# Four column groups for a gate projection, four row groups for the row broadcasts of a head

## The reference

```python
xm, z = jnp.split(h @ w_in, 2, axis=-1)
xc = jax.nn.silu(_conv_centred(xm, conv_w, conv_b))
q = _headwise(xc, wq); k = _headwise(xc, wk); v = _headwise(xm, wv)
gin = jnp.concatenate([q, k, v], axis=-1)
ipre = (jnp.einsum('btc,dch->dbht', gin, w_ig) + b_ig[:, None, :, None]).astype(F32)
lf = jax.nn.log_sigmoid((jnp.einsum('btc,dch->dbht', gin, w_fg) + b_fg[:, None, :, None]).astype(F32))
...
m_t = jnp.maximum(inter, jnp.max(dmat, axis=-1))
s = jnp.einsum('bhtd,bhsd->bhts', qc, kc) * jnp.exp(dmat - m_t[..., None])
w_inter = jnp.exp(inter - m_t)
h = num / jnp.maximum(jnp.abs(den), jnp.exp(-m_t))[..., None]
```

## Time and profile before

| | us |
|---|---|
| median of 3 runs | 1950.06 (1946.19 to 1950.61) |
| span of the profiled execution | 1948.8 |
| PE busy in it | 1816.9 (93%) |
| PE weight loads busy | 1050.9 (54%) |
| DVE, ACT, POOL busy | 604.2, 495.2, 167.7 |
| mean granted clock of PE | 0.968 of full speed |

### The profile page before, as it was taken

How to read it: one execution, slowest core, us unless ns; L and a number is a source line. 1 busy time by engine, 2 the same in 40 slices (tenths; PEclk the granted TensorE clock), 3 DMA queues, 4 the chain that set the end, 5 groups by cost and what they waited for, 6 DMA issues and landing times.

```text
span 1948.8 us, 16614 instructions
## 1 busy us (share of the span) xinstructions
PE 1816.9 (93%) x6421; PEld 1050.9 (54%) x6421; DVE 604.2 (31%) x979; ACT 495.2 (25%) x960; POOL 167.7 (9%) x158
## 2 busy tenths in 40 slices
PE   6899999999989899988989998999799998898998
PEld 3355534755655554546455455545455536575655
DVE  0333005336340202375320552321433005445420
ACT  2201323323320114343111222231201223433300
POOL 1000001001000000052043000000100001100100
PEclk9999998999999998999999997999899999999999
DMA  6522222233242321242365221323222221212122
GB/s 189 203 86 86 88 74 76 76 112 116 83 146 95 113 86 43 76 150 98 130 126 156 86 86 44 98 98 110 73 86 87 99 74 44 83 48 87 44 88 75
DMA packets 105140, 185.98 MB, mean 95 GB/s; under 512 B 5136, under 2 KB 54704, under 8 KB 105072
## 3 DMA queue, kind: packets, MB, share of 16 engines
q1 hardware_dynamic: 95816, 158.40, 24.2%
q0 software_dynamic: 8640, 26.46, 4.6%
q10 hardware_dynamic: 616, 0.16, 0.1%
HBM read 164.47 MB, written 20.54 MB: 95 GB/s over the span
## 4 chain that ended last, share of the span: by engine, by line
PE 88%; DVE 5%; ACT 3%; issue 1%; DMA 1%; SPq 0%; DVEq 0%; ACTq 0%; POOLq 0%
PE acc L500 69%; PE mix L500 17%; PE acc L565 1%; DMA out_new_C<-cst 1%; DVE hT L1523 1%; ACT cp L1276 1%; DVE mix L1344 1%; DVE rd L1505 1%; DVE cstat L1666 1%; PE mix L915 0%; DMA ring<-in_a_w_out 0%; DMA cst<-in_c_k_g 0%; DVE dx L1590 0%; DVE hT L1348 0%; DVE fqk L1626 0%
## 5 line engine op out<-in xcount | busy, mean ns | idle before, releaser
L500 PE MATMUL acc<-hT,ring 128*128 128x385 f32 x1664 | 548.3, 491 | 15.8 <-DVE hT L1351 14.4
L500 PEld LDWEIGHTS acc<-hT,ring 128*128 128x128 f32 x1664 | 317.9, 192 | 244.6 <-issue 21.9
L500 PE MATMUL acc<-z,ring 128*128 128x385 f32 x512 | 169.5, 492 | 6.1 <-DMA ring<-in_a_w_out 4.2
L500 PE MATMUL acc<-ring,sc 128*2 128x384 f32 x512 | 170.2, 486 | 1.6 <-ACT mst L992 1.2
L500 PEld LDWEIGHTS acc<-z,ring 128*128 128x128 f32 x512 | 97.9, 192 | 77.7 <-issue 6.1
L500 PE MATMUL mix<-qs,ring 128*128 128x256 f32 x512 | 117.6, 392 | 9.6 <-DVE qs L1507 9.6
L500 PEld LDWEIGHTS mix<-qs,ring 128*128 128x128 f32 x512 | 100.1, 197 | 27.6 <-issue 13.2
L500 PEld LDWEIGHTS acc<-ring,sc 128*2 128x2 f32 x512 | 41.3, 85 | 119.1 <-issue 112.2
L1363 DVE SCALAR_TENSOR_TENSOR y<-acc,modv,y 128x128 f32 x64 | 23.4, 413 | 223.8 <-PE acc L500 223.8
L500 PE MATMUL acc<-ring,hT 128*128 128x512 f32 x192 | 85.5, 608 | 0.0
L500 PE MATMUL acc<-xc,bd 128*128 128x385 f32 x128 | 57.5, 574 | 14.2 <-DVE hT L1523 8.4
(11 more groups left out here) (297 smaller groups left out, 2212.6 us busy)
## 6 DMA issues: line engine op xcount, KB each, us to landing
ring<-in_w_mod SPq DMA_DIRECT2D x64, 768.0 KB, 6.2
ring<-in_a_w_in SPq DMA_DIRECT2D x32, 1024.0 KB, 6.9
ring<-in_state_mlstm_C SPq DMA_DIRECT2D x16, 1024.0 KB, 7.8
out_new_C<-cst POOLq DMA_DIRECT2D x32, 512.0 KB, 3.2
ring<-in_a_w_out SPq DMA_DIRECT2D x16, 1024.0 KB, 7.8
ring<-in_c_w_in SPq DMA_DIRECT2D x16, 1024.0 KB, 7.6
ring<-in_b_w_in SPq DMA_DIRECT2D x12, 1024.0 KB, 6.3
ring<-in_b_w_out SPq DMA_DIRECT2D x4, 1024.0 KB, 6.2
```

Source lines behind the costliest of these rows:

```text
L500: return nc.tensor.matmul(out, lhsT=lhsT, rhs=rhs, start=start, stop=stop)
```

## The change

The gate projection gives product number f (of 16) to the output partitions 32 * (f mod 4) to 32 * (f mod 4) + 15, so that four partial sums form in four groups of columns of the array, in one bank. The first four products start the four sums, the wait for the convolution stands between the first 16 and the second 16 products, and the last four raise semaphores: three a new one, `gate_groups`, the last one `acc_ready`. ACT waits for both and copies all 128 partitions. `gsel` is 128 partitions tall with the selection repeated in the four groups, filled by four copies, so that the two products which spread the rows also add up the four partial sums.

`r_m` and `r_fl` become the two halves of one tensor `r_mf` of 128 partitions. Broadcast n of a head contracts over the 32 partitions from 32 * n alone. Each of the four raises `bcast_ready`, and ACT and DVE wait for four times as many.

```diff
-            r_m = sb("r_m", TC, rows=64, stack=st)
-            r_fl = sb("r_fl", TC, rows=64, stack=st)
+            r_mf = sb("r_mf", TC, stack=st)
...
+        r_m, r_fl = r_mf[0:64, :], r_mf[64:128, :]
-        grow = kw[1][0:16, 0:TC]
-        gsel = kw[1][0:16, TC:TC + P]
+        grow = kw[1][:, 0:TC]
+        gsel = kw[1][:, TC:TC + P]
...
                 for n in range(4):
-                    d = n % 2
-                    src = r_m if n < 2 else r_fl
-                    ins = mm(mix[:, seg((2 + n) * 512, TC)],
-                             ident[0:64, 32 * d + h:32 * d + h + 1].to_broadcast([64, P]), src[:, :], True, True)
-                ins.then_inc(bcast_ready, 1)
+                    r = seg(32 * n, 32)
+                    mm(mix[:, seg((2 + n) * 512, TC)], ident[r, seg(32 * n + h, 1)].to_broadcast([32, P]),
+                       r_mf[r, :], True, True).then_inc(bcast_ready, 1)
...
-                pairs = [(g4[:, f, 1, :], xm3[:, f, 1:1 + W]) for f in range(AT_)]
-                pairs += [(g4[:, f, 0, :], xc3[:, f, :]) for f in range(AT_)]
                 ps = bank(t)
-                for n, (a, b) in enumerate(pairs):
-                    if n == AT_:
-                        pe.wait_ge(xc_ready, AT_ * (ia + 1))
-                    ins = mm(ps[0:16, 0:W], a, b, n == 0, n == len(pairs) - 1)
-                ins.then_inc(acc_ready, 1)
+                for f in range(AT_):
+                    mm(ps[seg(32 * (f % 4), 16), 0:W], g4[:, f, 1, :], xm3[:, f, 1:1 + W], f < 4, False)
+                pe.wait_ge(xc_ready, AT_ * (ia + 1))
+                for f in range(AT_):
+                    last = f - (AT_ - 4)
+                    ins = mm(ps[seg(32 * (f % 4), 16), 0:W], g4[:, f, 0, :], xc3[:, f, :], False, last >= 0)
+                    if last >= 0:
+                        ins.then_inc(gate_groups if last < 3 else acc_ready, 1)
...
-                act.wait_ge(bcast_ready, H + 1)
+                act.wait_ge(bcast_ready, 4 * (H + 1))
...
+                act.wait_ge(gate_groups, 3 * (ia + 1))
                 ps = ready(tile("gate", l, 0))
-                nc.scalar.copy(grow[:, 0:P], ps[0:16, 0:P])
-                move(tile("gate", l, 0), grow[:, P:TC], lambda ps: ps[0:16, LAT:W])
+                nc.scalar.copy(grow[:, 0:P], ps[:, 0:P])
+                move(tile("gate", l, 0), grow[:, P:TC], lambda ps: ps[:, LAT:W])
...
-                nc.vector.tensor_copy(gsel.rearrange("p (n c) -> p n c", c=32)[:, :, 0:AH],
-                                      ident[0:16, 0:16].rearrange("p (n c) -> p n c", c=AH)).then_inc(gsel_ready, 1)
+                for q in range(4):
+                    r = seg(32 * q, 16)
+                    ins = nc.vector.tensor_copy(gsel[r, :].rearrange("p (n c) -> p n c", c=32)[:, :, 0:AH],
+                                                ident[r, r].rearrange("p (n c) -> p n c", c=AH))
+                ins.then_inc(gsel_ready, 1)
...
-                dve.wait_ge(bcast_ready, H + 1)
+                dve.wait_ge(bcast_ready, 4 * (H + 1))
```

More of the change, by code:

```diff
@@ L275, in trunk @@
         mod_ready = sem("mod_ready")
+        gate_groups = sem("gate_groups")
         gsel_ready = sem("gsel_ready")
```

## The result

The changed kernel takes 1899.74 us (median of 4, 1895.39 to 1904.55) against 1950.18 us before, a ratio of 0.9745 with a 95% interval of 0.9727 to 0.9763.

The account below looks back on a forecast made before the run. PE was taken to bound the kernel, busy 93% of the span; gate 20.1 and broadcasts 8.2 us sum to 28.3 us saved, 1950.1 - 28.3 = 1921.8 us, range 1904 to 1951.

Parts of the forecast that it names:

- What bounds: Whole kernel: PE busy 93% of the span; gate and broadcasts stand alone on its chain, 67 us at stake.
- The spacing: Gate and broadcast records: a slot is set by moving columns, about 0.323 us; a shape change costs about 0.1 us.
- The rival in which each change of group drains: Gate and broadcasts: going to another group costs like a shape change, 11 us slower, 1961 us; chance 0.11.
- The unknown overlap: Gate and broadcasts: whether neighbouring records on different groups overlap; gain between 0 and full, one half taken.
- the forecast of half: Gate and broadcasts: n products need n+1 slots, not 2n, if records start in program order; chance 0.48.
- The gate's term: Gate projection: 64 slots become 33 per layer, 10.0 us saved in each of two layers, 20.1 us.
- the full-overlap rival: Gate and broadcasts: all four groups run abreast, saving 31.1 and 12 us, sum 43, 1907 us; chance 0.14.
- The broadcasts: Row broadcasts: eight slots become five per head, 0.97 us in six heads, 1.2 in two first; 8.2 us.
- Its bound by weight loads: Broadcasts under full overlap: loads at 0.124 us each bound the stage at 1.19 in place of 2.58 us.
- The hidden edits: Gate's convolution wait, ACT's 128-partition copies and DVE's small preparation copies: 0; uncovered, the small copies would cost 0.5 us.
- The increments, put at 0: 30 semaphore increments added on PE: put at 0; at most 2.7 us, by the skill's price 0.8 us.
- The clock term: Layer 3's old-state and value products: low-clock stretches cost 1.68 us each and may move; +-5 us, middle 0.

Follow-up runs that it names:

- fours: Changed kernel, but four gate products in a row go to the same column group (f // 4), then four to the next: 1908.57 us, one execution.
- pairs: Changed kernel, but two gate products in a row go to the same column group (f // 2 mod 4): 1900.23 us, one execution.
- threes: Changed kernel, but three gate products in a row go to the same column group (f // 3 mod 4): 1908.03 us, one execution.
- the modulation: Changed kernel with the modulation's products of two weight columns, all four layers, also dealt to four column groups: 1817.64 us, ratio 0.9326.
- the kernel with rows of 64: Changed kernel, but a head's four broadcasts use two groups of 64 rows, both of one group first: 1901.62 us, one execution.

## Why the prediction was wrong, point by point

**What bounds.** Right. Both stages stood alone on the chain, and every microsecond that the trace shows gone in them is gone from the span.

**The spacing.** Right. A pass still takes 0.323 us on its group; the fours begin with four passes at that distance on one group. The rival in which each change of group drains fell at once: four passes start and end within 0.52 us, 0.03 more than one takes (the fence at 265.58 above), and only the changes of shape still cost 0.1 us.

**The unknown overlap: the step that failed.** "If records start in program order" was an assumption, said to be one, and the forecast of half hung on it alone. Pairs, threes and fours show that passes on different groups don't keep one order; each group has a line of its own, and with every fourth product on a group a full line leaves no other group without work. The gate's term was 20.1 us and measured 31.1, as the full-overlap rival had it. I had given that rival 0.14, with "each product's two passes on one group" against it; that reason is void. The Trainium skill, "TensorE: Matmul & The Clock Gate", Part 3, says the same of program order, and there the measurement differs: four passes start in the first 0.17 us of the gate of the pairs, among them that of the seventh product, while a second pass of the first has to wait 0.32 us. Its 3.07x for four row groups is near what the broadcasts show (2.77 / 0.95 = 2.9, with the changes of shape); its 2.38x for three column groups has no run here, four of them give 20.41 / 4.88 = 4.2.

**The broadcasts.** 8.2 us forecast, 15.9 measured, and the full-overlap rival's 12 was short too. Its bound by weight loads, one after another at 0.124 us, doesn't hold across groups: all eight loads pass within 0.31 us (the fence at 359.28 above). So two slots remain, 0.65 us, with 0.3 of shape changes and first load. In the two first heads the lower clock, which I scaled in, no longer touched them (0.86 us each). That was luck, worth 1.15 of the 15.9 us: with the same broadcasts it touched one of them again in the fours (1.47 us at a granted clock of 0.56) and in the threes (1.16 us at 0.72).

**The hidden edits.** Right. The convolution's wait, the wider copies and the four small copies cost nothing that shows. The increments, put at 0, cost a little: ACT's copy now starts 0.22 us after the end of the last gate record (268.18 + 2.77 to 271.17), before 0.09. It is 0.11 us in the fours, where ACT waits for the same two semaphores but the last passes of the groups end further apart, so the cost seems to come with increments that fall together.

**The clock term.** The middle of 0 was off by 6.6 us, past its bound of 5, because the term counted one stage alone: the products with the old state and the values in layer 3. The chain shows that stage in heads 0 to 3, to be held against the earlier trace rows: first heads 2 and 3 of the kernel before, then the changed kernel, the pairs and the fours.

```profile
1767.00 20.08 PE mix L500 x88
...
1828.60 20.07 PE mix L500 x88
```

```profile
1602.87 20.08 PE mix L501 x88
...
1662.61 18.40 PE mix L501 x88
...
1720.67 19.84 PE mix L501 x88
...
1780.17 18.40 PE mix L501 x88
```

```profile
1600.89 20.08 PE mix L501 x88
...
1660.64 18.40 PE mix L501 x88
...
1718.69 19.78 PE mix L501 x88
...
1778.13 20.08 PE mix L501 x88
```

```profile
1614.00 18.40 PE mix L501 x88
...
1672.06 18.40 PE mix L501 x88
...
1730.12 18.40 PE mix L501 x88
...
1788.18 18.40 PE mix L501 x88
```

18.40 us is the stage at the full clock. Before, three of the four heads had a stretch at the lower one; the changed kernel has two, the fours none. In this stage the change gave 1.9 us net, within the bound. The changed kernel and the pairs do the same work in the same time up to here and still differ in head 3, so where the stretches fall doesn't follow from the work of the stage alone. The same holds for the first heads. In layer 0 head 0's first 4 us on the broadcasts had a granted clock of 0.78; the changed kernel's have 1.00 (busy time by stretch: PE, PEld, DVE, ACT, POOL, granted clock, DMA share, GB/s):

```profile
291.00:295.00 4.00, 3.85 (x28) 3.07 (x29) 1.43 (x5) 2.29 (x7) 2.89 (x2) 1.00 0.00 0
295.00:300.00 5.00, 5.00 (x25) 4.38 (x24) 0.75 (x2) 1.21 (x2) 0.22 (x1) 1.00 0.00 0
```

That these stretches make up the 6.6 us is read from the traces, head by head (2.7 us in the first head of layer 0 behind its broadcasts, 1.0 in that of layer 3, 1.2 ahead of the two first broadcasts, none of which the term counted, and the 1.9 above); no run moved the clock by itself.

**The start.** The first gate record came 3.5 us later than before. In the six other runs with the modulation untouched it came between 262.1 and 264.1 us, and the kernel with rows of 64, whose code up to there is that of the changed kernel, has the earliest of the six (262.09), so this is spread. It is open what it comes from.

## What to carry to other kernels

Where a product fills 16 of 128 columns or 32 of 128 rows and many follow each other, dealing them to four groups can cut PE's time to a quarter, fp32 passes included (here the gate from 20.41 to 4.88 us; four broadcasts alone, with their shape changes, from 2.77 to 0.95), as long as not more than two products (four passes) in a row go to one group. Deal round robin or in pairs, not in longer blocks, let each group's last product raise a semaphore, and let the next product, which the partial sums need anyway, add them up. Look for such groups by the records and the shape in the groups by shape, not by how much code they are: here the modulation was worth more (82 us between the medians) than both stages of this change.

## What the runs showed of the hardware that I had not expected

- Passes of products on different groups start out of program order: 7 ns apart across four groups, while the second pass of the first waits 0.32 us for its group.
- Each column group behaves as a line of four passes: runs of one, two, three and four products in a row took 4.88, 4.92, 8.88 and 11.46 us for the same 64 passes, against 4.85, 4.85, 8.7 and 11.3 by that rule.
- Weight loads of 128 columns for different row groups run abreast: two passes on each of four row groups passed in 0.95 us with their loads and two changes of shape.
- Two groups of 64 rows have lines of their own too: eight passes in 1.50 us, with the second group's first product third in program order.
